# Column order and accumulator order of the weight products, layer by layer

## What is computed

```python
def even_layer(x, norm_g, w_in, ..., w_out):        # layer 0
    proj = rmsnorm(x, norm_g) @ w_in
    qa, ka, va, za, qb, kb, vb, ob, zb, gif = split_cols(proj, EV_SIZES)
    ...
    y = concatenate([ya, yb]) ; return y @ w_out    # x = x + this
# odd_layer: layer 1.  _layer_ab: layer 2.  _layer_c: layer 3, each of the same frame:
    h = jnp.matmul(_rmsnorm(x, norm_g).astype(x.dtype), w_in)
    ...
    return x + jnp.matmul(y.astype(x.dtype), w_out)
```

## Time and profile before

| | |
|---|---|
| median of 3 runs | 1913.26 us (1913.12 to 1914.15) |
| span of the profiled execution | 1911.3 us |
| TensorE matmul busy | 1901.8 us in 10370 matmuls |
| TensorE weight load busy | 1636.2 us (beside the matmuls) |
| VectorE, ScalarE, GpSimd busy | 1219.0, 1012.4, 170.1 us |
| moved by DMA | 340.25 MB, mean 178 GB/s |

### The profile page before, as it was taken

How to read it: one execution, slowest core, us unless ns; L and a number is a source line. 1 busy time by engine, 2 the same in 40 slices (tenths; PEclk the granted TensorE clock), 3 DMA queues, 4 the chain that set the end, 5 groups by cost and what they waited for, 6 DMA issues and landing times.

```text
span 1911.3 us, 26221 instructions
## 1 busy us (share of the span) xinstructions
PE 1901.8 (100%) x10370; PEld 1636.2 (86%) x10370; DVE 1219.0 (64%) x1688; ACT 1012.4 (53%) x1574; POOL 170.1 (9%) x142
## 2 busy tenths in 40 slices
PE   9999999999999999999999999999999999999998
PEld 7888888888889998898888888888888888888886
DVE  6655655555566887687557888645555778754553
ACT  7434445664557765764543345556454344446643
POOL 0000000110011111100001211000000111100110
PEclk9999999999999999999999999999999999999999
DMA  9555545545554444444565554554555555555453
GB/s 351 193 178 187 176 158 187 170 165 183 179 180 157 157 151 161 149 147 163 178 198 190 191 178 166 183 176 158 181 179 188 190 186 174 164 185 171 162 199 133
DMA packets 95033, 340.25 MB, mean 178 GB/s; under 512 B 10704, under 2 KB 11472, under 8 KB 94784
## 3 DMA queue, kind: packets, MB, share of 16 engines
q1 hardware_dynamic: 93536, 333.92, 52.4%
q0 software_dynamic: 944, 3.61, 0.6%
q10 hardware_dynamic: 432, 1.06, 0.1%
HBM read 336.44 MB, written 2.10 MB: 177 GB/s over the span
## 4 chain that ended last, share of the span: by engine, by line
PE 100%; ACT 0%; DVE 0%; issue 0%
PE ACC L736 18%; PE ACC L738 18%; PE ACC L737 18%; PE ACC L741 9%; PE ACC L744 9%; PE ACC L743 5%; PE ACC L742 5%; PE ACC L749 2%; PE ACC L750 2%; PE ACC L751 2%; PE PM L852 1%; PE PM L867 1%; PE PM L905 1%; PE PM L889 1%; PE PM L890 1%; PE PM L888 1%
## 5 line engine op out<-in xcount | busy, mean ns | idle before, releaser
L1441 DVE TENSOR_TENSOR WL<-RAW,WH 128x1024 fp32r<-128x1024 f32 (+1 forms) x624 | 791.8, 1284 | 534.3 <-ACT WH L1075 533.1
L1075 ACT ACTIVATE WH<-RAW 128x1024 fp32r<-128x1024 f32 (+1 forms) x626 | 650.7, 1052 | 508.9 <-PE ACC L738 264.9
L736 PE MATMUL ACC<-WH,XHL 128*128 128x512 f32 x1012 | 402.3, 397 | 0.0
L738 PE MATMUL ACC<-WH,XHL 128*128 128x512 f32 x1012 | 394.3, 390 | 0.0
L737 PE MATMUL ACC<-WL,XHL 128*128 128x512 f32 x1012 | 394.0, 389 | 0.0
L741 PE MATMUL ACC<-XHL,WH 128*128 128x512 f32 x768 | 307.9, 401 | 0.1
L744 PE MATMUL ACC<-XHL,WH 128*128 128x512 f32 x768 | 303.8, 396 | 0.0
L738 PEld LDWEIGHTS ACC<-WH,XHL 128*128 128x128 f32 x1012 | 190.0, 188 | 40.1
L737 PEld LDWEIGHTS ACC<-WL,XHL 128*128 128x128 f32 x1012 | 190.2, 188 | 38.6
L736 PEld LDWEIGHTS ACC<-WH,XHL 128*128 128x128 f32 x1012 | 190.1, 188 | 38.3
L743 PE MATMUL ACC<-XHL,WL 128*128 128x256 f32 x768 | 213.7, 278 | 0.0
(11 more groups left out here) (368 smaller groups left out, 2367.4 us busy)
## 6 DMA issues: line engine op xcount, KB each, us to landing
RAW<-in_w SPq DMA_DIRECT2D x621, 512.0 KB, 3.3
X<-in_x SPq DMA_DIRECT2D x4, 512.0 KB, 11.8
RAW<-in_w SPq DMA_DIRECT2D x6, 256.0 KB, 4.8
Y<-in_xT SPq DMA_DIRECT2D x2, 512.0 KB, 10.1
S<-in_bias POOLq DMA_DIRECT2D x8, 128.0 KB, 2.6
S<-in_od_gate_w POOLq DMA_DIRECT2D x1, 1024.0 KB, 6.1
S<-in_final_norm POOLq DMA_DIRECT2D x1, 1024.0 KB, 7.5
out<-Y SPq DMA_DIRECT2D x2, 512.0 KB, 2.6
```

Of the source, the lines that this page charges most:

```text
L736: e.matmul(o, th, hi[:, kk, :], start=f, stop=False)
L738: m = e.matmul(o, tl, hi[:, kk, :], start=False, stop=l)
L1075: e.activation(hi, src, ACT.Copy).then_inc(s_hi)
L1441: e.tensor_tensor(lo, src, hi.bitcast(F32), ALU.subtract).then_inc(s_lo)
```

## The change

The weights of token-major jobs of 512 columns are stored in another column order by `arrange`, and TensorE reads them with a stepped access pattern that undoes it, so that column i of the result is the same as before. The pattern is set by layer in SPREAD (number of parts, length of a run):
- Layer 0: the two halves of the 512 columns in turn. The reads go to word 0, 256, 1, 257, and so on.
- Layer 1: the two halves in turn in runs of 16 words.
- Layer 3: the four quarters in turn: word 0, 128, 256, 384, 1, and so on.
- Layer 2: the weights are not spread. In the token-major jobs the loops are exchanged: for each kt the accumulators take turns at every matmul (hi for t = 0, hi for t = 1, lo, lo, then the low input). In the wide jobs the 512 columns of input are read as 16 high, 16 low, 16 high and so on; the bank then holds runs of 16 of each in turn, the two matmuls of 256 columns write only the runs for the high input, and VectorE's reduction adds words 16 apart instead of 256.

Wide jobs of the other layers, mode "feat", and all plain fp32 work stay as they are. The outputs are written to a bank in contiguous order but for the two 256-column matmuls of layer 2's wide jobs.

```diff
+SPREAD = {0: (2, 1), 1: (2, 16), 3: (4, 1)}
+
+def spread_order(layer):
+    i = np.arange(512)
+    if layer not in SPREAD:
+        return i
+    parts, run = SPREAD[layer]
+    return (i // run % parts) * (512 // parts) + i // (run * parts) * run + i % run
+
+def spread_view(x, layer):
+    if layer not in SPREAD:
+        return x
+    parts, run = SPREAD[layer]
+    if run == 1:
+        return x.rearrange("p (a c) -> p c a", a=parts)
+    return x.rearrange("p (a g c) -> p g a c", a=parts, c=run)
...
         def halves_of(j):
+            if jobs[j].layer == 2:
+                return ACC[j % 2][:, :].rearrange("p (g h c) -> p g c h", g=32, h=2)
...
+                    elif J.mode == "tok" and J.layer == 2:
+                        halves = [slice(128 * t, 128 * t + 128) for t in range(2)]
+                        for t, c in enumerate(halves):
+                            e.matmul(acc[t], xh[:, c], hi[:, kk, :], start=f, stop=False)
+                        for t, c in enumerate(halves):
+                            e.matmul(acc[t], xh[:, c], lo[:, kk, :], start=False, stop=False)
+                        for t, c in enumerate(halves):
+                            m = e.matmul(acc[t], xl[:, c], hi[:, kk, :], start=False, stop=l)
                     elif J.mode == "tok":
+                        wh, wl = spread_view(hi[:, kk, :], J.layer), spread_view(lo[:, kk, :], J.layer)
                         for t in range(2):
                             th, tl, o = xh[:, 128 * t:128 * t + 128], xl[:, 128 * t:128 * t + 128], acc[t][:, 0:w]
-                            e.matmul(o, th, hi[:, kk, :], start=f, stop=False)
-                            e.matmul(o, th, lo[:, kk, :], start=False, stop=False)
-                            m = e.matmul(o, tl, hi[:, kk, :], start=False, stop=l)
+                            e.matmul(o, th, wh, start=f, stop=False)
+                            e.matmul(o, th, wl, start=False, stop=False)
+                            m = e.matmul(o, tl, wh, start=False, stop=l)
+                    elif J.mode == "wide" and J.layer == 2:
+                        (wh0, wh1), (wl0, wl1) = ((w[:, kk, 0:128], w[:, kk, 128:256]) for w in (hi, lo))
+                        both = XHL3[:, kt, :].rearrange("p (h g c) -> p g h c", h=2, g=16)
+                        high = [a.rearrange("p (g h c) -> p g h c", g=16, h=2)[:, :, 0, :] for a in acc]
+                        e.matmul(acc[0], wh0, both, start=f, stop=False, skip_group_check=True)
+                        e.matmul(high[0], wl0, xh, start=False, stop=l, skip_group_check=True)
+                        e.matmul(high[1], wl1, xh, start=f, stop=False, skip_group_check=True)
+                        m = e.matmul(acc[1], wh1, both, start=False, stop=l, skip_group_check=True)
...
+                    summed = S[s][:, 512 * J.b:512 * J.b + 512].rearrange("p (g c) -> p g c", g=32) if J.layer == 2 else dst
+                    e.tensor_reduce(summed, halves_of(j), AX, ALU.add).then_inc(s_evD)
...
+        if J.mode == "tok" and J.n == 512:
+            spread = _np.empty_like(x)
+            spread[:, spread_order(J.layer)] = x
+            x = spread
```

More of the change, by code:

```diff
@@ L727, in products @@
                         for t in range(2):
-                            e.matmul(acc[t], xh[:, 128 * t:128 * t + 128], hi[:, kk, :], start=f, stop=False)
-                            e.matmul(acc[t], xl[:, 128 * t:128 * t + 128], hi[:, kk, :], start=False, stop=False)
+                            e.matmul(acc[t], xh[:, 128 * t:128 * t + 128], spread_view(hi[:, kk, :], 0), start=f, stop=False)
+                            e.matmul(acc[t], xl[:, 128 * t:128 * t + 128], spread_view(hi[:, kk, :], 0), start=False, stop=False)
@@ L730, in products @@
                         e.wait_ge((s_lo0, s_lo)[kk], p + 1)
                         for t in range(2):
-                            m = e.matmul(acc[t], xh[:, 128 * t:128 * t + 128], lo[:, kk, :], start=False, stop=l)
+                            m = e.matmul(acc[t], xh[:, 128 * t:128 * t + 128], spread_view(lo[:, kk, :], 0), start=False, stop=l)
+                    elif J.mode == "tok" and J.layer == 2:
[6 more added lines that the diff above has]
+                            m = e.matmul(acc[t], xl[:, c], hi[:, kk, :], start=False, stop=l)
@@ L766, in last_products @@
                             th, tl = (x[kt // 8][:, kt % 8, 128 * t:128 * t + 128] for x in (YH8, YL8))
-                            e.matmul(o, th, hi[:, kk, :], start=False, stop=False)
-                            e.matmul(o, th, lo[:, kk, :], start=False, stop=False)
-                            m = e.matmul(o, tl, hi[:, kk, :], start=False, stop=p == NP - 1 and kk == nk - 1)
+                            wh, wl = spread_view(hi[:, kk, :], 3), spread_view(lo[:, kk, :], 3)
+                            e.matmul(o, th, wh, start=False, stop=False)
+                            e.matmul(o, th, wl, start=False, stop=False)
+                            m = e.matmul(o, tl, wh, start=False, stop=p == NP - 1 and kk == nk - 1)
                         if t:
@@ L1488, in evacuate @@
                     e.wait_ge(s_mm, p + 1)
-                    e.tensor_reduce(dst, halves_of(j), AX, ALU.add).then_inc(s_evD)
+                    summed = S[s][:, 512 * J.b:512 * J.b + 512].rearrange("p (g c) -> p g c", g=32) if J.layer == 2 else dst
+                    e.tensor_reduce(summed, halves_of(j), AX, ALU.add).then_inc(s_evD)
                     e.wait_ge(s_row, J.layer + 1)
```

## The result

The changed kernel takes 1969.76 us (median, 1969.71 to 1969.90) against 1913.7 us (now the median of four executions): a ratio of 1.029, with an interval of 1.028 to 1.031. It is slower, by 56 us. The profiled execution has a span of 1967.8 us, 56.5 more than before, and 2.0 us lie around it again.

What follows compares the result with a forecast made beforehand. TensorE bounds the kernel, by matmuls times the distance between starts. 1913.3 us plus 599 for layers 0 and 3, all other terms zero, gave 2513 us; range 1908 to 2880 us.

Steps and rivals of the forecast that it cites:

- The bound, the count, the carry-over: Whole kernel: TensorE sets the time, matmul count times step; counts stay; span changes reach the median one to one.
- Layers 0 and 3, a lone column costs two slots: 2880 token-major matmuls of layers 0 and 3: 435 ns a step, 208 more than 227, 599 us in all.
- the row of plain fp32: Profile row of a plain fp32 product, 0.84 ns a column; basis for taking 435 ns per 512 columns.
- The row of the reduction over two halves: VectorE's PSUM reduction reading words 1 KB apart at 1.06 ns an element: hops free there, but 2.5 times slower than TensorE.
- The fixed share of 13 ns: Every matmul: some 13 ns beyond its columns, alike for 512 and 256, so no price on reading or adding a column.
- Rival 5: Changed products: new orders drop the fixed share, 13.5 ns each, 76 us faster, 1837 us; chance 0.03.
- Rival 2: Two streams held open but not four: layer 0 free, layer 3 at 435 ns, 2153 us; chance 0.10.
- Layer 1: 576 token-major matmuls in runs of 16: taken as zero; one slot lost per run would be 7.7 us.
- Layer 2, wide: Wide products reading and writing runs of 16: taken as zero; one slot a run would be 10 us together.
- Layer 2, accumulators in turn, and the reduction: Layer 2: switching accumulator and stationary tile costs 0; VectorE's reduction stays at 1.22 us and covered.

Runs made afterwards that it cites:

- e1: Changed kernel with two halves in turn, word by word, in token-major products of all layers, layer 2's own edits undone: 1863.4 us, 0.974 of the kernel before.
- e4: As e1, but four places 256 bytes apart (layer 0), eight 256 bytes apart (1), four 64 bytes apart (2), every second word (3): 2464.5 us.
- e9: As e1, but layer 0 words 0, 256, 4, 260; layers 1, 2 neighbouring pairs 8, 4 words apart; layer 3 runs of four 8 apart: 2698.8 us.
- e3: As e1, two words in turn, but 512 bytes apart in layer 0, 256 in layer 1, 64 in layer 2, 16 in layer 3: 1863.0 us.
- e2: As e1, two halves in turn, but in runs of 2 words (layer 0), 4 (layer 1), 8 (layer 2) and 32 (layer 3): 2136.9 us.
- e8: Changed kernel with two halves in turn in layer 3 in place of four quarters, the rest kept: 1894.1 us, 0.990 of the kernel before.
- e7: Changed kernel with only layer 2's edits kept (accumulators in turn, wide jobs in runs of 16): 1918.2 us, 1.0022 of the kernel before.
- e6: As e1, but words 0, 256, 2, 258 (layer 0), every fourth word (1), eight places 16 bytes apart (2), 0, 2, 1, 3 (3): 2339.2 us.
- e5: e1 plus input columns read two in turn, 512 bytes apart, in wide and feature-major products: 1829.5 us, 0.956 of the kernel before.

## Why the prediction was right or wrong

- **The bound, the count, the carry-over:** right. The time is matmuls times steps; 4608 x 11 ns gave e1's time, and no other engine or wait became the limit (TensorE waits 2.9 us in the changed kernel).
- **Layers 0 and 3, a lone column costs two slots (+208 ns):** wrong, and this is the step that failed. It put layer 0 at +359 us, measured -17, and layer 3 at +240, measured +62.5. The steps were 216 and 283 ns in place of 435. A step near 435 does exist, 451 ns (e4, e9), for orders that leave a line after one word, but that is luck as far as the runs show: the argument of two slots a column gives neither the 461 of words two lines on nor the 269 to 329 of other orders that take one word a visit. What was wrong was to count neighbours in the order of the whole stream. In the model above each of two readers sees every second column; halves in turn are then the best order and plain order only the second. The Trainium skill, "SBUF — State Buffer", Specifications (TRN2), asks for at least two hits per 16-byte line for full bandwidth. The runs agree in part, once the hits are counted for each reader of the model: one hit a visit took 269 to 487 ns, two took 227 to 250 and four 216, so two were still 11 ns short of the best. Layer 0 looked like a breach of the rule only because I counted along the stream. The Trainium skill, "Vector Engine (DVE) Microarchitecture Reference", section 5.2, has for VectorE one stream that alternates between two regions 16 KiB apart at full rate, and runs of two neighbours with free hops between them. The first held for TensorE at the distances tried, 16 bytes to 1 KB (e1, e3: 216 ns); the second did not (e2, 329 ns; e9, 451 ns).
- **Which row I went by.** The sum was taken from the row of plain fp32, which gave the price of a case that the change did not have. The row of the reduction over two halves was an order of just this kind with no penalty, and I set it aside as too slow to tell. It pointed the right way for layer 0, but not to a gain.
- **The fixed share of 13 ns:** I concluded that it was no price on reading, since it did not grow with the columns. The conclusion was wrong: 11 of the 13 ns go with the order of reads alone. What did not follow from "the same for 256 and 512 columns" is that the order has no part in it.
- **Rival 5** was nearly right on what an order can give back (13.5 ns a product against 11 in e1), at a chance of 0.03, but it sought the share at the start of a stream or in the bank. **Rival 2** had the right shape, two places free and four not, with a price of 56 ns instead of 208. The measured kernel is a mix of the two, and no rival was a mix. The range 1908 to 2880 us held 1969.8, and "slower" was right, but the way that it was slower was not the one foretold: layer 0, which was to carry 359 of the 599 us, gained, and e8 shows that halves in layer 3 would have made the whole change a gain. The forecast of +599 us was ten times the +56 that came.
- **Layer 1:** taken as zero with a bound of 7.7 us; measured 6.7, the bound rather than the value. That one slot for each run fits so well is luck: by that price runs of 4 would cost 53 ns, and they cost 23 (e2). **Layer 2, wide:** taken as zero with a bound of 10 us; measured 4.2 (e7). The Trainium skill, "PSUM — Partial Sum Buffer", Specifications (TRN2), says that any non-contiguous pattern slows matmuls significantly. Here a product that writes runs of 16 took at most 3 ns more (118 against 115 and 117, e7). **Layer 2, accumulators in turn, and the reduction:** zero, right (227 ns in e7; 1223 ns for the reduction in the changed kernel).

**What stays open.** The two readers are a model that was fitted to the runs up to e6 and then foretold e9; no run shows them as such. In every order tried the even and the odd columns walk alike, so the runs can't tell two readers from one that takes the columns two at a time; an order in which only the odd columns leave their lines wasn't tried. Why two words from a line cost 11 ns in a product of 512 columns, about 8 in a feature-major one of 256, and nothing like twice as much for twice the columns, is not explained; nor is the ladder 269, 283, 329, 451 among orders that all take one word a visit, beyond that coming back to one of two lines is cheaper than going on to a new one, while turning among four (480, 487) is not. Whether the weight loads beside the stream have a part wasn't tried.

## What to carry to other kernels

Where TensorE is the bound and its reduced fp32 products step some 227 ns for 512 columns, read the moving side from two places in turn, word by word (16 bytes to 1 KB apart were tried), and permute the stored operand or the reading of the accumulator to match: 11 ns a product, and with the input's products (e5) 4.4% of this kernel in the end. Four or eight places in turn, pairs in turn, and every second word of one place all cost more than plain order here. When a row prices a pattern, check that it is the same pattern for the unit that fetches, not only for the stream; and when a change puts a different edit into each layer, measure one window for each layer, since the total hid a gain of 17 us in one under a loss of 74 in the others.

## What the runs showed of the hardware

- Plain order is not the fastest for a reduced fp32 stream from SBUF: 227 ns for 512 columns, 216 with two places in turn (213.3 are the columns at the granted clock of 1.00).
- In these runs the price goes with what every second column does: pairs of neighbours four words apart (0, 1, 4, 5) are as slow as every second word, 451 ns, though both words of a pair lie in one line.
- The time of such a stream spans 216 to 487 ns with the same words, the same count and the same clock, and neither the busy share nor the waits show it; only the steps between starts do.
